# Where the two operands of a matmul lie in SBUF: offsets of panels and activations, and the order of the three passes

## The reference

```python
h = rms_norm(x, pre_norm_g[l]); proj = h @ w_in[l]               # first block
x = x + rms_norm(jnp.concatenate([ya, yb], axis=-1) @ w_out[l], post_norm_g[l])
p = h @ even_w_in; h = h + jnp.concatenate([a_out, r_out], -1) @ even_w_out
q, k, v = jnp.split(h @ odd_w_in, 3, axis=-1); h = h + attention @ odd_w_out
h = h + (jax.nn.silu(conv(h @ w_gate)) * (h @ w_up)) @ w_down
```

## Time and profile before

| | |
|---|---|
| median of three runs | 2301.74 us (2298.83 to 2303.05) |
| the profiled execution, its own time | 2309.54 us |
| its span, first to last instruction | 2307.8 us |
| granted TensorE clock, mean over the span | 0.982 of full speed |
| TensorE matmul | 2217.0 us busy, 96% of the span, 14840 matmuls |
| weight loads | 1974.6 us, 86% |
| VectorE, ScalarE, GpSimd | 1129.9 us (49%), 966.7 us (42%), 620.7 us (27%) |
| DMA | 175.64 MB, mean 76 GB/s |

### The profile page before, as it was taken

The page is one execution under the profiler, slowest core; times in us unless marked ns, Lnnn a source line. Parts: engine busy times, 40 slices in busy tenths (PEclk is TensorE's granted clock), DMA queues, the critical chain, the costliest instruction groups (busy, mean ns, idle before and its releaser), DMA issues. The chain is left out here.

```text
span 2307.8 us, 35487 instructions
## 1 busy us (share of the span) xinstructions
PE 2217.0 (96%) x14840; PEld 1974.6 (86%) x14840; DVE 1129.9 (49%) x1684; ACT 966.7 (42%) x1404; POOL 620.7 (27%) x480
## 2 busy tenths in 40 slices
PE   8999999998999999998999999999999989999998
PEld 6887579886589987886899999998988879988987
DVE  3458635557452234796444434444555534433443
ACT  4346634356543335435433313334655533322332
POOL 2112320123214325337123302322333212320321
PEclk8999999999999989999999999999999999999999
DMA  6341023310122212130233233222111013324322
GB/s 191 125 149 50 0 74 102 94 53 6 38 78 92 74 47 62 55 121 4 68 96 91 77 107 95 80 86 82 38 56 56 19 56 92 92 78 114 92 82 74
DMA packets 235315, 175.64 MB, mean 76 GB/s; under 512 B 7704, under 2 KB 230160, under 8 KB 234644
## 3 DMA queue, kind: packets, MB, share of 16 engines
q1 hardware_dynamic: 234836, 173.20, 25.2%
q10 hardware_dynamic: 320, 0.17, 0.0%
HBM read 171.20 MB, written 10.09 MB: 79 GB/s over the span
## 5 line engine op out<-in xcount | busy, mean ns | idle before, releaser
L347 DVE TENSOR_TENSOR panel_lo<-panel_raw,panel_hi 128x2048 fp32r<-128x2048 f32 (+2 forms) x148 | 332.0, 2243 | 252.7 <-ACT panel_hi L340 252.6
L340 ACT ACTIVATE panel_hi<-panel_raw 128x2048 fp32r<-128x2048 f32 (+2 forms) x150 | 266.8, 1778 | 368.2 <-PE product L450 252.6
L450 PE MATMUL product<-scaled_hi,panel_hi 128*128 128x256 f32 (+2 forms) x1232 | 282.4, 299 | 2.6 <-PEq L506 1.4
L450 PE MATMUL product<-scaled_hi,panel_lo 128*128 128x256 f32 (+2 forms) x1232 | 282.5, 299 | 0.0
L450 PE MATMUL product<-scaled_lo,panel_hi 128*128 128x256 f32 (+2 forms) x1232 | 282.2, 299 | 0.0
L450 PEld LDWEIGHTS product<-scaled_hi,panel_hi 128*128 128x128 f32 x1232 | 200.7, 188 | 11.5 <-issue 2.9
L450 PEld LDWEIGHTS product<-scaled_hi,panel_lo 128*128 128x128 f32 x1232 | 198.4, 188 | 7.4
L450 PEld LDWEIGHTS product<-scaled_lo,panel_hi 128*128 128x128 f32 x1232 | 198.2, 189 | 6.7
L463 PE MATMUL product_banks<-panel_hi,scaled_hi 128*128 128x256 f32 x696 | 194.7, 280 | 0.0
L463 PE MATMUL product_banks<-panel_hi,scaled_lo 128*128 128x256 f32 x696 | 194.4, 279 | 0.0
L463 PE MATMUL product_banks<-panel_lo,scaled_hi 128*128 128x256 f32 x696 | 194.4, 279 | 0.0
(11 more groups left out here) (599 smaller groups left out, 5440.9 us busy)
## 6 DMA issues: line engine op xcount, KB each, us to landing
panel_raw<-in_w_in_dram SPq DMA_DIRECT2D x26, 1024.0 KB, 5.4
panel_raw<-in_ffn_w_gate_dram SPq DMA_DIRECT2D x44, 512.0 KB, 4.0
panel_raw<-in_ffn_w_up_dram SPq DMA_DIRECT2D x44, 512.0 KB, 5.3
panel_raw<-in_ffn_w_down_dram SPq DMA_DIRECT2D x32, 704.0 KB, 4.7
panel_raw<-in_even_w_in_dram SPq DMA_DIRECT2D x21, 1024.0 KB, 5.3
panel_raw<-in_odd_w_in_dram SPq DMA_DIRECT2D x12, 1024.0 KB, 5.2
panel_raw<-in_w_out_dram SPq DMA_DIRECT2D x8, 1024.0 KB, 6.2
panel_raw<-in_even_w_out_dram SPq DMA_DIRECT2D x8, 768.0 KB, 5.3
```

Of the source, the lines that this page charges most:

```text
L340: act.activation(panel_view(c.hi[g % 2], product), raw_view(c.raw[g % 2], product), ACT.Copy).then_inc(c.hi_made.sem, 1)
L347: dve.tensor_tensor(panel_view(c.lo[g % 2], product), raw_view(c.raw[g % 2], product), panel_view(c.hi[g % 2], product).bitcast(F32), ALU. ...
L450: done = pe.matmul(banks[b], weight(w, k), a[:, k, u:v], start=(k == 0 and x == 0), stop=(k == chunks - 1 and x == 2))
```

## The change

Three things are changed. No instruction is added or taken away.

1. The start offsets of the activation tensors are chosen anew, in several stages with another offset for the low part than for the high part, and the panels get places in their slots: `Segment(..., at)` gives a start in elements for high and low panel, and `panel_view` adds it (`FLAT_AT` is 0 bytes, `OUT_AT` 64, `WIDE_AT` 96, `PAIR_AT` 192, `VALUES_AT` 64 for the high part and 0 for the low one).
2. In T tiles the order of the three passes becomes high x high, low weight x high activation, high weight x low activation; in the odd layer's N tiles low panel, high panel, high panel with low activations. `row_tile`, `tail_tile` and `chunk` keep their order.
3. The `rstd` column of one norm (the one made ahead of the odd layer) moves out of its own allocation into the row of `eps`, so that nothing shifts the offsets behind it.

```diff
-SCALED_PHASES = {0: 64, 1: 64, 4: 64, 5: 64, 6: 192, 7: 192}
+SCALED_PHASES = {0: (96, 96), 1: (96, 96), 4: (96, 96), 5: (160, 224), 6: (160, 224), 7: (0, 64)}
 Y_PHASES = (0, 0)
-EVEN_Y_PHASE, QUERY_PHASE = 192, 192
-INNER_PHASES = (192, 0)
+EVEN_Y_PHASES, QUERY_PHASES = (160, 224), (224, 32)
+INNER_PHASES = ((160, 224), (0, 0))
+FLAT_AT, OUT_AT, WIDE_AT, PAIR_AT, VALUES_AT = (0, 0), (16, 16), (24, 24), (48, 48), (16, 0)
...
-    c.eps = sb("eps", [P, 1])
+    c.small = sb("small", [P, 8])
+    c.eps = c.small[:, 0:1]
...
+    def views(self, g):
+        c, (product, seg, _, _) = self.c, self.list[g]
+        return tuple(panel_view(t[g % 2], product, at) for t, at in zip((c.hi, c.lo), seg.at))
...
-def panel_view(slot_tile, product):
-    rows = slot_tile[:, 0:product.chunks * product.pitch].rearrange("p (k n) -> p k n", k=product.chunks)
-    return rows[:, :, 0:product.cols]
+def panel_view(slot_tile, product, at=0):
+    first = max(at + product.cols - product.pitch, 0)
+    rows = slot_tile[:, first:first + product.chunks * product.pitch].rearrange("p (k n) -> p k n", k=product.chunks)
+    return rows[:, :, at - first:at - first + product.cols]
...
 def wide_tile(...):
-        for x, (w, a) in enumerate(((w_hi, act_hi), (w_hi, act_lo), (w_lo, act_hi))):
+        for x, (w, a) in enumerate(((w_hi, act_hi), (w_lo, act_hi), (w_hi, act_lo))):
...
     # first_products: T segments of the opening product WIDE_AT, its N segments and w_out FLAT_AT;
     # the two late segments stay without one
     # even_products: retention and value N segments FLAT_AT, selected T segments PAIR_AT
     # odd_products: third N segment VALUES_AT, out OUT_AT; ffn_products: down FLAT_AT, the rest (0, 0)
...
-                        for x, (w, a) in enumerate(((w_hi, parts.hi), (w_hi, parts.lo), (w_lo, parts.hi))):
+                        order = ((w_lo, parts.hi), (w_hi, parts.hi)) if tile.kind == "N" else ((w_hi, parts.hi), (w_lo, parts.hi))
+                        for x, (w, a) in enumerate((*order, (w_hi, parts.lo))):
```

More of the change, by code:

```diff
@@ L413, with __init__ @@
 class Segment:
-    def __init__(self, panels, load, tiles, take):
-        self.panels, self.load, self.tiles, self.take = panels, load, tiles, take
+    def __init__(self, panels, load, tiles, take, at=(0, 0)):
+        self.panels, self.load, self.tiles, self.take, self.at = panels, load, tiles, take, at
 class Product:
@@ L3203, in odd_products @@
             tiles = [("H", j, half) for j in range(2) for half in range(2)] if third < 2 else [("N", u) for u in block_starts(TOK)]
-            segments.append(Segment(1, columns(w_in, 1024 * third + 256 * group, 256), tiles, None))
+            segments.append(Segment(1, columns(w_in, 1024 * third + 256 * group, 256), tiles, None, VALUES_AT if third == 2 else (0, 0)))
     into = Product(c, KD, 256, segments, step=STEP)
-    out = Product(c, KD, 256, [Segment(4, columns(w_out, 0, 256), T_tiles(), add_to_h(c, 2))], step=STEP)
+    out = Product(c, KD, 256, [Segment(4, columns(w_out, 0, 256), T_tiles(), add_to_h(c, 2), OUT_AT)], step=STEP)
     return into, out
@@ L3713, in odd_layer @@
     with ExitStack() as layer:
-        q = [c.sb(f"q_{part}", [P, KD, TOK], F32R, into=layer, phase=QUERY_PHASE) for part in ("hi", "lo")]
+        q = [c.sb(f"q_{part}", [P, KD, TOK], F32R, into=layer, phase=phase) for part, phase in zip(("hi", "lo"), QUERY_PHASES)]
         odd_stage(c, into, q, taken, ahead)
@@ L3766, in __init__ @@
         self.total = c.sb("square_total", [P, self.tiles * P if whole else tokens], into=stage)[:] if total is None else total
-        self.rstd = c.sb("rstd", [P, NB2], side=side, into=stage if held is None else held)
+        self.rstd = c.sb("rstd", [P, NB2], side=side, into=stage if held is None else held)[:] if rstd is None else rstd
         self.pending = 0
@@ L3861, in __init__ @@
         self.c, self.src, self.gain, self.tokens, self.pending = c, src, gain, tokens, 0
-        self.hi, self.lo = (c.sb(f"scaled_{n}", [P, KD, room or tokens], F32R, side, into=stage, phase=SCALED_PHASES.get(gain))
-                            for n in ("hi", "lo"))
+        self.hi, self.lo = (c.sb(f"scaled_{n}", [P, KD, room or tokens], F32R, side, into=stage, phase=phase)
+                            for n, phase in zip(("hi", "lo"), SCALED_PHASES[gain]))
     def act_hi(self, act, k):
```

66 lines of the change are left out of this document (33 added, 33 removed).

## The result

Nine executions of the changed kernel have a median of 2317.88 us (2310.49 to 2321.33), nine of the kernel before, the three from ahead of the prediction among them, 2304.94 us (2298.83 to 2312.95). The ratio is 1.0051, with a 95% interval of 1.0037 to 1.0066: the change makes the kernel slower by about 12 us. I had forecast 2275 and a range of 2262 to 2306: the time moved the other way and lies outside the range.

The account below looks back on a forecast made before the run. TensorE's matmul stream, busy 96% of the span, was taken as the bound. Terms 2.8 + 9.9 + 17.0 = 29.7 us, less a tenth, 26.7, from the median 2301.7 gave 2275 us, range 2262 to 2306.

Parts of the forecast that it names:

- nothing else moves: Whole kernel: same matmuls, counts, DMAs and waits, so only the pitch between TensorE's matmuls changes; nothing gained or lost elsewhere.
- terms 6 and 7: Splits into shifted places stay hidden behind TensorE; the order of passes and the moved `rstd` cost nothing: nothing for either.
- Term 1: First block's 512-column T tiles: distance between moving operand and next weights becomes 0, 226.7 ns a matmul, 2.8 us gained.
- Term 2: 256-column N tiles, odd layer's included: all reach 113.3 ns, 9.9 us gained; other end 5.0 us lost.
- My upper end: N tiles' unfavourable case: all go to 118.3 ns, 840 x 5.0 + 1656 x 0.5 = 5.0 us lost.
- Term 3: T pairs, feed-forward 0, even and odd layers: three quarters of 22.7 us, 17.0 gained; other end 12.4 lost.
- wrong in sign: Check set beforehand: feed-forward 0, which carries most pairs, passing 121 ns a matmul; 117 to 118 was expected, from 120.8.
- Term 4: Feed-forward 1, gate and up, 156.3 ns: at most 7.8 us gained or 3.4 lost; taken as nothing.
- Term 5: Late panels, 256 matmuls, and the chunkwise openings: unknown offsets, 1.2 us each way; taken as nothing.
- the slower one: Rival: collisions grow as operand distance nears 128, so 160 is no better or worse; 14.6 us slower, 2316; chance 0.16.
- History, not distance: Rival: streams fall into one of two rhythms and keep it; the change only draws anew, 12.8 us gained, 2289; chance 0.22.
- The rule against the change: Skill's rule: independent read ports, loading the next weights costs the running matmul nothing; no distance matters, time stays 2301.7.

Follow-up runs that it names:

- the second execution: Second profiled run of each kernel with no edit: 2309.82 us for the kernel before, 2321.38 us for the changed kernel.

## Why the prediction was wrong

**What bounds the kernel**, the pitch as the thing to read, and the step "nothing else moves" (terms 6 and 7) held: same counts, same splits, same waits. Order of passes: no price seen in any pitch. The sum started from 2301.74, the median of three runs; the median of nine is 2304.94, so 3.2 us of the miss lie in the start and not in a term.

**Term 1, 512 columns, forecast 2.8 us gained.** Held: 226.6 in the window, 1.0 to 2.2 us gained by excess, less in the second execution because the kernel before then had part of these tiles at 229.0. But the price of 233.1 was not one of d alone: it is what d = 64 costs behind N tiles in the long rhythm. With only this term in the kernel the N tiles behind gave the gain back.

**Term 2, N tiles, forecast 9.9 us gained.** This step failed in sign. I took the gain "since 113.3 has been seen on just this form", but the form was at 192, and the change moved it to 160. There the measured pitches are 118.6 in most of the kernel, 120.0 in one execution's retention, and 117.3 or 118.7 in streams: no stream and no stage showed 113.3 at that distance. The loss is 6.3 us against the first execution of the kernel before and 11.5 against the second. My upper end, 5.0 lost, was too small because I took the split of long and short N tiles in one profile (1656 and 840) for a property of the program. It was one draw: in the second execution 1184 of the retention's 1344 were short. The odd layer's share, 2.4 us gained, did not come either: 2.1 us of excess before and after. The other end of a term whose size differs between executions must be counted from the most favourable of them, here all 2304 matmuls and the 192 of the tails: 2496 x 5.3 = 13.2 us.

**Term 3, pairs, forecast 17.0 us gained.** Failed in size for the even layer (1.6 ns a matmul of the 4.9 over the floor; 0.9 to 1.3 us in place of my 3.1 x 3/4 = 2.3) and in sign for the rest: 121.4 in place of 120.8 in feed-forward 0, and the odd layer's T up by 1 us; together 3 us lost. The mark I had set for "wrong in sign", feed-forward 0 past 121, came. The premise was "wherever d is the same in all passes and the tile has one width, the pitch is at the floor or one step above it", from which I took that a constant distance is what matters. The streams show what matters is which distance: constant 160 puts N at 117.3 or 118.7 and pairs at 120.0, constant 96 puts pairs at 123.3. The trace of before had said so: 512 columns at a constant 64 at 233.1, and even pairs at a constant 64 at 121.8, *above* feed-forward 0, whose distance changes. I used these two as reasons to leave 64, not as evidence against constancy.

**Term 4, feed-forward 1**: 156.5 against 156.3, 0.2 us lost; "nothing" held. Term 5 was not resolved.

**The rivals.** The one that came nearest in time was the slower one, 14.6 us lost against 12.9 by the medians, to which I gave 0.16. But its mechanism, the nearer to 128 the worse, is refuted: N at 128 takes 118.7, at 96 and at 0 120.0. Its price was right by luck, two errors that cancel: it gave pairs 12.4 us, measured about 2 net, and N tiles 5.0, measured 6 to 11. "History, not distance" was half of the truth, and I gave it 0.22. In the streams alone the distance decides which rhythms there are and the stream ahead picks among them; the draw it spoke of was real, but at 160 the rhythm of 113.3 was never seen.

**The rule against the change.** The Trainium skill ("TensorE: Matmul & The Clock Gate", Part 2) has the weight load and the moving operand on independent read ports. Streams of nothing but matmuls at full clock, which differ in one operand's offset alone, run at 113.3 to 120.3 ns for 256 columns and at 226.7 to 234.2 for 512. And the pitch of N is the same whether activations or panels are moved to a distance. So the running matmul does depend on where the weights that are loaded meanwhile lie, and the rule's 2301.7 was wrong too; that the two reads meet in a port or a bank is my guess, and nothing measured says where.

**What would have been the better forecast.** With one more doubt, that 160 is simply unseen, terms 2 and 3 are open on both sides and the sum is near zero with 10 us each way. The trace of before said one thing more: its first 512-column tiles (from 33 us, where the clock is full, to 40) and its late panels, at the same d = 64 as the 233.1, ran at 228.9. A profiled execution 7.8 us above the median of its own kernel was the sign that the execution, not the program alone, sets a part of the time; that the rhythms and the granted clock differ between executions came out of the second profiles.

## What to carry to other kernels

A price read at one operand offset holds for that offset: an offset that no row shows needs a stream of its own before the kernel is arranged around it, and such a stream takes 5 to 11 us of running. Where two windows of one program show two pitches for the same instruction, take a second profile before counting how many have which, and compare the time at half clock along with the pitches; and judge such a change by medians of many executions, since here two profiled executions differed by 1 us and the medians by 13. A short rhythm that depends on what ran before is no firm gain, and a change that only aims at it can as well remove it.

## What the runs showed of the hardware that I had not expected

- The pitch of back-to-back matmuls depends on the byte offsets of both operands: 512 columns 226.7 ns at d = 0 and 234.2 at 160; N of 256 columns 113.3 at best and 120.3 at worst. For N it is the distance that counts, whichever operand is moved. Moves by multiples of 256 bytes (up to 1792) changed nothing in streams that were in the long rhythm.
- At some offsets there are two or three stable rhythms: 113.3, 116.9 and 117.8 (N at 192), 113.3 and 117.8 (N at 64), 117.3, 118.7 and 120.0 (N at 160), 228.9 and 233.3 (512 columns at 64), 119.1 to 119.5 and 121.3 to 121.4 (pairs at 32 and 64). A stream keeps the one it began with for whole tiles, and in a quiet program the stream ahead decides it the same way every time. In the kernel N and 512-column streams that followed each other directly did as the streams alone in 24 of 26 cases; behind other work the same stage was in one rhythm in one execution and in the other in the next.
- Offsets found the fastest alone did not carry over: (32, 64) took 119.1 to 119.5 alone, 119.1 in the even out and 121.4 in feed-forward 0.
- No pair of 256 and 272 columns reached the floor at any of the 128 combinations tried, each entered once, neither with operands that move by 64 bytes from chunk to chunk nor at constant offsets; the best was 119.1 against 116.9.
- Two executions of one program that differ by 5 us in the pitch of their N tiles took the same time within 0.3 us; they stood 102 us (short rhythm) and 82 us (long) at half clock.
